# Two transformer blocks on one core: a new order of the scan, scores beside values, and the time steps computed with keys and values

## The reference

```
proj = rmsnorm(x) @ w_in           # z 2048, xbc 4096, dt 64, q 1024, k 256, v 256, gates 2048
xbc  = silu(depthwise_conv(xbc))   # 5 taps; split into xs (8 groups x 4 heads x 64), b, c (8 groups x 128)
dt   = softplus(dt_raw + dt_bias)  # (tokens, 2 directions, 32 heads)
y    = ssd_scan(xs, dt_fwd, a_fwd, b, c) + flip(ssd_scan(flip(xs), flip(dt_bwd), a_bwd, flip(b), flip(c)))
       + xs * d_skip               # per group: y_diag = (c b^T * decay) @ (xs * dt), y_off from the other chunk's state
y    = gated_rmsnorm(y, z) @ w_out
attn = window_attention(q, k, v)   # 16 heads, softmax with a sink over 256 keys
x    = x + norm((sigmoid(g) mix of both) @ w_o);  x = x + norm(relu(h @ w_mlp_in)^2 @ w_mlp_out)
```

## Time and profile before

| | before |
|---|---|
| median of 3 runs | 942.24 us (942.22 to 942.31) |
| profiled execution: time, span | 942.23 us, 940.4 us |
| PE busy | 932.4 us, 99% of the span |
| PEld, DVE, ACT, POOL busy | 86%, 70%, 54%, 6% |
| DMA | 166.51 MB, mean 177 GB/s |
| granted TensorE clock | full after the start |

### The profile page before, as it was taken

One profiled execution on the slowest core, in us unless ns is written; L12 is line 12 of the kernel. 1 busy time (PEld: TensorE's weight loads), 2 busy tenths in 40 slices (PEclk: granted clock), 3 DMA queues, 4 the chain that ended last, 5 costly groups with the idle time before them and its releaser, 6 DMA issues.

```text
span 940.4 us, 13246 instructions
## 1 busy us (share of the span) xinstructions
PE 932.4 (99%) x5362; PEld 807.9 (86%) x5362; DVE 662.4 (70%) x946; ACT 507.6 (54%) x664; POOL 60.8 (6%) x68
## 2 busy tenths in 40 slices
PE   9999999999999999999999999999999999999998
PEld 8988899988888888888888888899888898888887
DVE  6779789998878764778776446767665758776433
ACT  6457876676555733456554335755653455554331
POOL 1000000023321000000003310000000000000000
PEclk9999999999999999999999999999999999999999
DMA  8943233554224475435447955353355435546551
GB/s 306 341 168 124 93 133 135 180 167 169 91 90 157 140 307 197 169 131 221 179 180 236 256 196 206 136 205 128 123 217 179 179 135 217 187 179 224 178 179 45
DMA packets 25278, 166.51 MB, mean 177 GB/s; under 512 B 2987, under 2 KB 3115, under 8 KB 6657
## 3 DMA queue, kind: packets, MB, share of 16 engines
q1 hardware_dynamic: 22464, 156.12, 46.1%
q0 software_dynamic: 2752, 9.54, 3.5%
HBM read 164.57 MB, written 1.08 MB: 176 GB/s over the span
## 4 chain that ended last, share of the span: by engine, by line
PE 86%; DVE 11%; ACT 2%; issue 1%; ACTq 0%; DVEq 0%
PE ps L393 54%; PE ps L582 11%; PE ps L587 6%; DVE conv_acc L1688 5%; DVE w_lo L1455 3%; PE ps L843 1%; PE ps L772 1%; PE ps L787 1%; PE ps L424 1%; PE ps L426 1%; PE ps L433 1%; PE ps L512 1%; PE ps L630 1%; PE ps L893 1%; PE ps L852 1%
## 5 line engine op out<-in xcount | busy, mean ns | idle before, releaser
L1455 DVE TENSOR_TENSOR w_lo<-raw,w_hi 128x2048 fp32r<-128x2048 f32 x145 | 331.3, 2291 | 181.0 <-ACT w_hi L1075 180.8
L1075 ACT ACTIVATE w_hi<-raw 128x2048 fp32r<-128x2048 f32 x145 | 275.5, 1906 | 179.1 <-PE ps L393 160.2
L393 PE MATMUL ps<-w_hi,ht 128*128 128x512 f32 (+1 forms) x576 | 181.4, 388 | 0.0
L393 PE MATMUL ps<-ht,w_hi 128*128 128x256 f32 (+1 forms) x816 | 150.6, 286 | 0.0
L393 PEld LDWEIGHTS ps<-ht,w_hi 128*128 128x128 f32 (+1 forms) x816 | 126.2, 190 | 4.1 <-issue 4.0
L393 PEld LDWEIGHTS ps<-w_hi,ht 128*128 128x128 f32 x576 | 107.3, 188 | 22.4 <-issue 1.1
L393 PE MATMUL ps<-ht,w_lo 128*128 128x256 f32 (+1 forms) x408 | 115.3, 282 | 0.0
L393 PE MATMUL ps<-w_lo,ht 128*128 128x512 f32 (+1 forms) x288 | 110.5, 384 | 0.0
L582 PE MATMUL ps<-ht,w_hi 128*128 128x512 f32 x448 | 109.5, 391 | 0.0
L393 PE MATMUL ps<-w_hi,ff_hi 128*128 128x512 f32 x256 | 99.7, 389 | 0.0
L393 PE MATMUL ps<-w_lo,ff_hi 128*128 128x512 f32 x256 | 99.6, 389 | 0.0
(11 more groups left out here) (301 smaller groups left out, 1217.4 us busy)
## 6 DMA issues: line engine op xcount, KB each, us to landing
raw<-in_w_stream SPq DMA_DIRECT2D x145, 1024.0 KB, 4.8
bias<-rel_scratch POOLq DMA_DIRECT2D x1, 3072.0 KB, 21.2
bias<-in_rpb POOLq DMA_DIRECT2D x16, 128.0 KB, 7.9
x_first<-in_x_in SPq DMA_DIRECT2D x2, 512.0 KB, 4.1
raw<-in_w_stream SPq DMA_DIRECT2D x2, 512.0 KB, 6.4
gates<-in_gate_bias POOLq DMA_DIRECT2D x4, 256.0 KB, 6.0
gates<-in_gate_bias POOLq DMA_DIRECT2D x2, 512.0 KB, 7.2
x<-in_x_in POOLq DMA_DIRECT2D x1, 1024.0 KB, 5.3
```

What stands on the lines that cost most here:

```text
L393: ins = pe.matmul(o, still, moving, start=first and n == 0, stop=last and n == 2, skip_group_check=True)
L1075: act.activation(split_home(s)[0][:, 0:width(s)], raw[s % RAW_RING][:, 0:width(s)], ACT.Copy).then_inc(hi_ready, 1)
L1455: dve.tensor_tensor(lo[:, 0:width(s)], raw[s % RAW_RING][:, 0:width(s)], hi[:, 0:width(s)].bitcast(F32), ALU.subtract).then_inc(lo_ready, 1)
```

## The change

Eight edits, which the prediction calls by these letters.

- A. The dt piece (slot 2) goes; keys, values and dt become one matrix of 576 columns, in slots 2, 3 and 4, with 3, 3 and 2 of its 8 row tiles. Values and dt are one product with 320 moving columns. The transposes of dt go.
- B. `scores` moves from the end of a slot into `slot_middle`, behind `values1`; the same in slots 94 to 97.
- C. `conv_turn` of chunks 2 and 4 uses banks 6 and 7.
- D. The logarithm of dt is cut into four parts, in DVE's slots 7, 8, 11 and 12.
- E. The scan's 32 masking matmuls (L867) go. DVE instead copies the backward direction's exponents over the forward ones in PSUM, under a mask (`ssd_choose`, COPY_PREDICATED), and ACT takes one exponential instead of two.
- F. So the diagonal lacks one direction: `make_twins` multiplies b and c on DVE, 16 matmuls with one moving column (`twin_sums`) sum them, `own_terms` adds them to `d_skip`, and `ssd_skip` takes the place of L1720.
- G. In slots 28 to 36 DVE follows `scan_slot`: `w_lo` is made one slot ahead, not two, in slots 29 to 38, and slot 39 makes two.
- H. ACT takes the SiLU of two z chunks at once in slot 31, and loads its table of the exponential earlier.

```diff
 STRETCHES = [
-    ("q", S_Q, "feat", 2), ("dt", S_DT, "dt", 1), ("q", S_DT + 1, "feat", 2), ("kv", S_KV, "kv", 2), ...
+    ("q", S_Q, "feat", 2), ("kv", S_KV, "kv", 3), ("q", S_Q1, "feat", 2), ...
...
+            def stream_kv(s):
+                part, opens, closes = slots[s][3:]
+                hi, lo = w_hi[s % SPLIT_RING], w_lo[s % SPLIT_RING]
+                tiles = tiles_of(part)
+                pe.wait_ge(lo_ready, s + 1)
...
+                        ins = three(ps[:, keys, i * TOK:i * TOK + TOK], ht_hi[:, kt, :], ht_lo[:, kt, :],
+                                    hi[:, c], lo[:, c], True, i == 0 and kt == 0, kt == 7)
...
+                        ins = three(ps[:, 6 + r, 0:KV_COLS - 256], ht_hi[:, kt, tokens], ht_lo[:, kt, tokens],
+                                    hi[:, c], lo[:, c], False, kt == 0, kt == 7)
...
             def conv_turn(c):
-                    claim(key, 4 + r)
+                    claim(key, 4 + 2 * (c in (2, 4)) + r)
...
             def ssd_decay(g, c):
                 for d in range(2):
                     key = ("decay", g, c, d)
                     claim(key, 5 + d)
                     pe.matmul(ps[:, 5 + d, :], cum_s[g % 2][:, 2 * c + d, :], cum_l[c][:, d, :, :],
-                              start=True, stop=False)
-                    pe.matmul(ps[:, 5 + d, :], unit[:, :], far[:, d].unsqueeze(1).to_broadcast([P, PER_GROUP, P]),
-                              start=False, stop=True).then_inc(*fill_of(key))
+                              start=True, stop=True).then_inc(*fill_of(key))
+            def twin_sums():
+                claim("twins", 4)
+                pe.wait_ge(twins_ready, 4)
...
+                        ins = pe.matmul(ps[:, 4, at0:at0 + 1], twins[2 * c + g // 4][:, g % 4, :], tri[:, 0, P - 1:P],
+                                        start=True, stop=True)
...
             def slot_middle(s):
                 if 0 <= s - 10 < 8:
                     values1(s - 10)
+                if 0 <= s - 7 < 8:
...
+                    scores("a1", s - 7, lambda h: q_t[:, tile + h, :], lambda h: k_t[:, tile // 4, :])
...
                 if 0 <= s - 28 < GROUPS:
                     ssd_decay(s - 28, 1)
+                    if s == 29:
+                        twin_sums()
...
             def decay_exps(g, c):
+                key = ("decay", g, c, 0)
+                emptied(act, ("decay", g, c, 1))
...
+                act.activation(decay[g % 2][c][:, :, :], ps[:, 5, :].rearrange("p (h l) -> p h l", h=PER_GROUP),
+                               ACT.Exp).then_inc(*drain_of(key))
...
+                if s == 31:
...
+                    act.activation(zg_half[1][:, :, :], zg_half[1][:, :, :], ACT.Silu).then_inc(z_last_silu, 1)
+                    act.preload_act_table(ACT.Exp)
...
+            def ssd_choose(g, c):
+                ready(dve, ("decay", g, c, 0)), ready(dve, ("decay", g, c, 1))
+                both = [ps[:, 5 + d, :].rearrange("p (h l) -> p h l", h=PER_GROUP) for d in range(2)]
+                dve.copy_predicated(both[0], tri[:, 2].bitcast(I32).unsqueeze(1).to_broadcast([P, PER_GROUP, P]),
+                                    both[1]).then_inc(*drain_of(("decay", g, c, 1)))
             def ssd_weigh(g, c):
-                link(dve.tensor_tensor(w[:, :, :], w[:, :, :], decay_back[c][:, :, :], ALU.add))
+            def make_twins():
+                dve.wait_ge(conv_silu, 8)
...
+            def scan_slot(s):
+                g, last = s - 28, s - 29
+                if g < GROUPS:
+                    ssd_choose(g, 0)
+                    ssd_weigh(g, 0)
+                if last > 0:
+                    ssd_skip(last)
+                if g < GROUPS:
+                    ssd_choose(g, 1)
+                if last == 0:
+                    own_terms()
+                    ssd_skip(0)
+                if g == 0:
+                    make_twins()
+                else:
+                    split_lo(s + 1)
+                if g < GROUPS:
+                    ssd_weigh(g, 1)
+                if s == S_GATE + 5:
+                    dve.wait_ge(gate_bias_second, 32)
+                    gate_bias(1)
+                if last >= 0:
+                    ssd_gate(last)
...
             for s in range(SLOTS):
+                if 28 <= s <= 36:
+                    scan_slot(s)
...
+                if 37 <= s <= 39:
+                    split_lo(s + 1)
-                if s + AHEAD < SLOTS and s != S_Q2 - 1 and not late:
+                if s + AHEAD < SLOTS and s != S_Q2 - 1 and not late and not 28 <= s < 39:
                     split_lo(s + AHEAD)
...
             def decay_rows(g):
                 if g >= 2:
-                    ready(pool, ("decay", g - 2, 1, 0))
+                    ready(pool, ("decay", g - 2, 1, 1))
```

More of the change, by code:

```diff
@@ L127, with tiles_of @@
 ]
+def tiles_of(part):
+    return range(KV_TILES * part, min(KV_TILES * part + KV_TILES, 8))
 def slot_table():
@@ L655, in stream @@
                     return
[L656 to L666, removed]
                 for half in range(2):
@@ L1017, in _, with width @@
                     mix_turn(1)
+        def width(s):
+            return len(tiles_of(slots[s][3])) * KV_COLS if slots[s][0] == "kv" else PIECE
         piece_of = []
@@ L1309, in _ @@
                                    ACT.Copy).then_inc(cum_hi_ready, 1)
+                if 0 <= s - 29 < GROUPS:
+                    key = ("state", s - 29)
+                    ready(act, key)
+                    act.activation(state[:, :, :], ps[:, 7, :].rearrange("p (a b) -> p a b", a=2),
+                                   ACT.Copy).then_inc(*drain_of(key))
+                if 0 <= s - 28 < GROUPS:
+                    decay_exps(s - 28, 1)
+                if s == 31:
+                    for c in (2, 3):
+                        emptied(act, ("z", c, 0)), emptied(act, ("z", c, 1))
+                    act.activation(zg_half[1][:, :, :], zg_half[1][:, :, :], ACT.Silu).then_inc(z_last_silu, 1)
+                    act.preload_act_table(ACT.Exp)
                 if 0 <= s - 30 < GROUPS:
@@ L1711, in ssd_weigh @@
                                   ALU.mult).then_inc(decay_scaled, 1)
+            def make_twins():
+                dve.wait_ge(conv_silu, 8)
+                for c in range(RT):
+                    for half in range(2):
+                        first, tokens = 4 * half, slice(c * P, c * P + P)
+                        dve.tensor_tensor(twins[2 * c + half][:, :, :], bc[:, first:first + 4, tokens],
+                                          bc[:, GROUPS + first:GROUPS + first + 4, tokens],
+                                          ALU.mult).then_inc(twins_ready, 1)
@@ L2101, in _ @@
             pool.wait_ge(cum_s_ready, GROUPS)
-            ready(pool, ("decay", GROUPS - 1, 1, 0))
+            ready(pool, ("decay", GROUPS - 1, 1, 1))
             for cols, done in ((slice(512, 1024), gate_bias_second), (slice(1024, 2 * D), gate_bias_rest)):
```

247 lines of the change are left out of this document (132 added, 115 removed).

## The result

The changed kernel takes 947.11 us (median of 5 executions, 945.79 to 947.38) against 942.22 us before (942.14 to 942.31): ratio 1.0045, 95% interval 1.0033 to 1.0056. It is slower by 4.9 us, where 938.3 us was forecast and the range ended at 942.6. The profiled execution took 947.31 us with a span of 945.5.

The account below looks back on a forecast made before the run. PE, busy for 99% of the span, was taken as the bound. From 942.23 us, 11.35 us removed and 7.5 us added gave net -3.9 us, 938.3 us, with a range of 934.0 to 942.6.

Parts of the forecast that it names:

- A: Slots 2 to 4, keys, values and dt as one matrix: PE does 1.7 us less, bounds 3.1 and -2.3.
- B: Scores moved from between transposes, in six slots and the second block: 0.9 us saved on PE, bounds 0 and 1.6.
- C: Convolution's transposes: the 0.6 us wait goes; of a 0.85 us gap in PE, 0.7 us gained by the end of slot 27.
- E, steady slot: Scan: 32 masking matmuls of 0.23 us go, 7.4 us in all; a steady slot falls from 11.37 to 10.45 us.
- wait in slot 28: PE newly waits 1.8 us, once, for bank 5 before the second decay matmul, behind DVE's low part and masked copy.
- gaps in slots 29, 30: PE's wait at the first c b^T of slot 30 and a 0.3 us gap beside it go: 0.65 us saved.
- F, the sums: 16 one-column matmuls on PE, priced at 0.10 us each from eight with 32 columns: 1.6 us added, from 0.4 to 3.7.
- wait at slot 40: PE stands 4.1 us at slot 40 because DVE makes its low part behind gates' bias and first `yt_lo`.
- R1: Rival: the wait at slot 40 drops PE to 1.2 GHz, 2.7 us more, 941.0 us; chance 15%.
- R2: Rival: no wait at slot 40, the sigmoid earlier or the low part elsewhere, 934.2 us; chance 10%.
- R3: Rival: DVE or POOL becomes the bound of the scan by a little, about 2 us, 940.3 us; chance 17%.
- R4: Rival: the masked copy takes two passes, 1.4 us, so DVE's scan slot is 11.3 us; 944.1 us; chance 10%.

Follow-up runs that it names:

- e9: Changed kernel with the scores put back between the two turns of the probabilities; 948.31 us, one execution; slot 2 to first c b^T 179.08 us against 178.66.
- e10: Changed kernel with all conv turns in banks 4 and 5 again; 944.52 us, one execution; slot 2 to first c b^T 178.74 us against 178.66.
- e2: Changed kernel with one matmul of 16 columns in place of the sixteen one-column sums, own terms left wrong; 940.07 us median, ratio 0.9979 to the kernel before.
- e5: Changed kernel with the sixteen sums put four at a time behind groups of three wide matmuls in slot 29; 943.80 us median, ratio 1.0015 to the kernel before.
- e8: Changed kernel with sums spread, slot 40's low part between gates' bias and first `yt_lo`, slot 29's behind the first choosing; 937.68 us median, ratio 0.9944 to before.
- b1: Kernel before with sixteen one-column fp32 matmuls, read by nothing, added in the middle of slot 29; 949.96 us median, ratio 1.0074 to the kernel before.
- e6: Changed kernel with slot 40's low part made in slot 38, behind the gates' bias and ahead of the first `yt_lo`; 941.76 us median, ratio 0.9992 to before.
- e1: Changed kernel with slot 40's low part made in slot 38, right behind slot 39's and ahead of the gates' bias; 942.45 us median, ratio 0.9993 to before.

## Why the prediction was wrong

The sum was 8.8 us too low. By its own steps, predicted against measured in the profiles:

| step | predicted | measured | from |
|---|---|---|---|
| A, B, C to the first c b^T | -3.3 | -2.35 | 203.33 to 200.98 |
| of which A | -1.7 | -1.9 | slot 2 to slot 7 |
| of which B (with slots 94 to 97) | -0.9 | -0.4 (without) | e9 |
| of which C | -0.7 | -0.1 | e10 |
| E, steady slot | 10.45 | 10.41 | stretch 228.05 to 280.10 |
| wait in slot 28 | +1.8 | +1.1 | waits |
| gaps in slots 29, 30 | -0.65 | about 0 | e2: 11.21 with one sum |
| F, the sums | +1.6 | +3.6 | 213.30 to 216.91 |
| clock in slot 29 | none | +4.2 | 18.89 - 14.66 (e5) |
| wait at slot 40 | +4.1 | +4.15 | timeline of PE |
| clock behind it | rival R1, +2.7 | +1.6 | changed and e8, from the eighth c b^T to the end |

For the last row: the changed kernel takes 945.5 - 280.1 = 665.4 us from there, e8, with full clock, 934.7 - 275.05 = 659.65. Of the difference of 5.75 the wait is 4.15.

The misses (of the three parts the sum alone) are 0.95 - 0.7 + 0.65 + 2.0 + 4.2 + 1.6 = 8.7 of 8.8 us.

**The step that failed is F.** It said "the nearest are the eight with 32 columns: 68.84 - 68.03 = 0.81 us, 0.10 each". The row counts eight records, but the loop in the code issues four matmuls: fp32 operands make two records each. One costs 0.20, so 16 would cost 3.2, and they measured 3.6. The upper bound of 3.7 us held. The number in the row should have been held against the loop; fp32r matmuls, such as slot 2's, and transposes count one for one, and that hid the difference.

**The larger half is the clock in slot 29, which the prediction didn't have at all.** It asked only where PE would stand. e2 and b1 show that 3.6 us of one-column matmuls, with PE busy throughout, end in the half clock. The rule that the prediction cited from the Trainium skill ("TensorE: Matmul & The Clock Gate", Part 1) is on an idle PE; at slot 40 the trace agrees with it (4.15 us of standing, then 1.2 GHz in part of 320 to 330). In slot 29 PE had been busy without a gap since 205.89, for 10.8 us, when the clock fell, and in b1 it waits for nothing between 195 and 240.

**The mechanisms that were right:** the wait at slot 40 with its place, order and size, the pace of the steady slot, the 0.68 us copy, the 0.15 us of 320 columns (0.146, from five matmuls between 29.29 and 30.02). A's 1.7 us was near the 1.9 measured. R2, R3 and R4 fell.

**What was partly right or mis-sized:** R1 happened, at 1.6 us instead of 2.7, with a chance of 15% put on it. The size is not a constant: in e5's profile, behind the same wait, the same sum (942.6 - 275.93 against 659.65, less 4.1) gives 2.9. The start, from which the price was taken, is no firm measure either: the profile gives a granted clock of 1.00 there, so the lower clock is read from the pace of the matmuls alone, and in the changed kernel the same 12 take 4.67 us, which would have priced R1 at 1.9. B was worth about half of its term, as far as measured, and C almost nothing, since DVE's full row sets when the SiLU for the turn of c = 4 can start. The prediction had seen that DVE has no idle time there, but looked for the loss at the end of slot 27 and took off 0.15 for it. The wait in slot 28 was forecast too long because PE was moved up by 0.6 us and DVE's low part left at 204.36, where both moved: to 202.04 on DVE, 2.3 us earlier.

## What to carry to other kernels

Hold the count of a row against the loop in the code before you divide by it: here an fp32 matmul was two records, a transpose or an fp32r matmul one. Price a run of narrow matmuls like a wait of PE: 3.6 us of them brought TensorE to 1.2 GHz with the engine fully busy, and between wide matmuls the same sums cost no more and left the clock full in that slot (profiles of e5 and e8). When a step is moved behind an engine's long wait, look at what follows it in that row; here one line in the right place (gates' bias, then low part, then `yt_lo`) was worth 5.4 us at the median (e6). Before a single execution is compared at a late point, subtract what it was already late at an early one.

## What the runs showed of the hardware that was not expected

- The clock falls without idle time: PE busy 5.00 of 5.00 us at clock 0.67 and 0.50. The cost of such a fall in slot 29 was 4.2 us in the changed kernel; in b1's executions the sums and the fall together cost from 4.6 to 8.2 us.
- The same program differs in how long the clock stays down. In e1 the mean clock was 0.999 at 938.41 us, 0.996 at 940.7 to 942.6, 0.994 or 0.995 at 942.5 to 943.0.
- A sum over one column takes as long as one over 32: 3.61 and 3.70 us for sixteen in fp32. So the columns aren't what is paid for; whether it is the weight load or the instruction stays open.
- A predicated copy of 128x512 in PSUM with an int32 mask took 0.68 us, the same as a plain sum of that size.
